# FFN down products as seven block products, with their sums on VectorE, and all operand buffers moved by 384 bytes

## The chip, the cores and the metric

The kernel runs on one core of a Trainium2 chip. Its metric is device time in microseconds (us). The engines in this text are TensorE (PE), VectorE (DVE), ScalarE (ACT), GpSimd (POOL) and the DMA queue that SyncE (SP) feeds.

## The reference

Three blocks for 256 tokens of width 1024: a sparse-attention layer and an MLA layer, each with a squared-ReLU MLP, and a hybrid mLSTM and windowed-attention layer, which ends in the FFN that this change is about. All is float32.

```python
hf = rmsnorm(x, norm_ffn_g)
x = x + (jax.nn.silu(hf @ w_gate) * (hf @ w_up)) @ w_down      # w_gate, w_up: 1024x2816; w_down: 2816x1024
...
return rmsnorm(x, norm_final_g)
```

## The kernel before

All of it is one program with an instruction list per engine, written out by hand, that wait for one another on semaphores. Weights stream through in chunks of 128x2048 float32 (1 MB), each loaded into one of two `raw` buffers. ACT copies a chunk to a rounded fp32r value (`whi`, helper `split_one`, L1566), and DVE (L2125, helper `low_part`) or POOL (L1535) writes the rest, raw minus whi, to `wlo`. Activations are split the same way, and each product is three matmuls on PE (high by high, high by low, low by high; lines 548 to 550 in `three`).

The last FFN runs over D_FF2 = 2816 in 11 steps of 256 columns: a gate chunk g(p), an up chunk u(p) and a down chunk d(p). PE makes g(p+1) and u(p+1), each 2 tiles x 8 k x 3 = 48 matmuls of 256 columns (`wide_step`), and then the down products of step p, 2 token blocks x 2 halves x 2 k x 3 = 24 matmuls of 512 columns (`ffn_down`, `down_products`). The down products of all steps add up in banks 0 to 3 of PSUM. Gate tiles lie in banks 4 and 5, up tiles in 6 and 7, two of each so that DVE can read one while PE fills the other. The steps run in a loop of 4 turns with two steps each, with two steps ahead of it and one behind.

Between the products, DVE multiplies the gate by the norm's row scale (L2763), ACT applies SiLU (L2073), DVE multiplies by up (L2769), ACT copies the rounded hidden value to `xC` (L2077), and DVE writes its rest (L2773). The norm ahead of the FFN is late: the products begin on gained but unscaled values, and DVE makes the scales while PE works on g0 and u0 (L2158 to L2164). PE spreads them to a row (L1343), and ACT copies that. The residual sum takes the same scales at the end (`residual_add`, L2138), followed by the final norm (ACT squares at L1552, POOL gain products at L1543, DVE scaling at L2183).

SP issues the chunk loads in order. Each waits until the low part of the chunk that was in its `raw` buffer is written.

## Time and profile before

| | us |
|---|---|
| median of 3 runs (lowest, highest) | 1139.35 (1138.67, 1140.9) |
| the profiled execution | 1141.42 |
| its span | 1139.6 |
| PE busy in the span | 1112.0 |
| DVE busy | 707.6 |
| ACT busy | 583.6 |
| POOL busy | 142.6 |

The profiled execution took 1.8 us more than its span, and 2.1 us more than the median. Sums made on the trace are differences within the span, so they can be taken from the median as they are. Busy time of PE counts matmuls that overlap in the pipeline. How fast it goes is read from the distance between the starts of two matmuls.

### The profile page before, as it was taken

To read this page: it belongs to the slowest core of one execution; us is meant where nothing else is said; L and a number is where in the kernel's file an instruction comes from. 1 tells how busy PE (TensorE), PEld (TensorE's weight loads), DVE (VectorE), ACT (ScalarE), POOL (GpSimd) and SP (SyncE) were. 2 spreads that over 40 slices of the span, in tenths; PEclk is the share of its full clock that TensorE was granted. 3 is DMA by queue.
4 is the path that set the end of the run, shared out by engine and by line. 5 is a ranking of instruction groups with operands and counts; after the bars stand their busy time and mean duration, and the time that the engine had idled before them with its cause. 6 is when DMAs were issued, how large, how long until landed. Compare 5 with 4: busy or idle time off the path is not lost.

```text
span 1139.6 us, 17781 instructions
## 1 busy us (share of the span) xinstructions
PE 1112.0 (98%) x7033; PEld 984.8 (86%) x7033; DVE 707.6 (62%) x997; ACT 583.6 (51%) x767; POOL 142.6 (13%) x105
## 2 busy tenths in 40 slices
PE   8899999999998999999999999999999999999997
PEld 7767888888887888888888999898899989999996
DVE  5764565565668646565656878566587566554554
ACT  5565544444579554444455546455555346443443
POOL 3543300000265240000030000000000011000001
PEclk9999999999999999999999999999999999999999
DMA  7917565555442236556545654436643545656552
GB/s 216 306 54 186 182 198 188 200 190 184 118 137 88 98 111 222 191 186 201 189 156 185 204 171 149 132 128 223 203 159 120 185 148 160 221 175 194 189 172 89
DMA packets 138782, 193.96 MB, mean 170 GB/s; under 512 B 7147, under 2 KB 112840, under 8 KB 138716
## 3 DMA queue, kind: packets, MB, share of 16 engines
q1 hardware_dynamic: 126796, 181.92, 48.4%
q10 hardware_dynamic: 11312, 11.05, 3.6%
q8 instruction: 45, 0.74, 0.3%
q0 software_dynamic: 608, 0.08, 0.1%
q14 instruction: 21, 0.17, 0.0%
HBM read 191.90 MB, written 6.37 MB: 174 GB/s over the span
## 4 chain that ended last, share of the span: by engine, by line
PE 83%; ACT 6%; DVE 5%; issue 2%; DMA 2%; POOL 0%; ACTq 0%; DVEq 0%; POOLq 0%
PE psum L548 20%; PE psum L549 20%; PE psum L550 20%; PE psum L709 11%; PE psum L710 5%; ACT arena L1552 3%; PE psum L637 2%; ACT whi L1566 2%; DVE wlo L2125 1%; DMA raw<-in_a_w_in 1%; PE psum L1264 1%; PE psum L668 1%; PE psum L1237 1%; DVE arena L2566 1%; DMA raw<-in_b_w_o 0%
## 5 line engine op out<-in xcount | busy, mean ns | idle before, releaser
L1566 ACT ACTIVATE whi<-raw 128x2048 fp32r<-128x2048 f32 (+2 forms) x174 | 325.9, 1875 | 255.5 <-PE psum L550 172.5
L2125 DVE TENSOR_TENSOR wlo<-raw,whi 128x2048 fp32r<-128x2048 f32 (+1 forms) x149 | 337.5, 2267 | 184.1 <-ACT whi L1566 183.2
L548 PE MATMUL psum<-xA,whi 128*128 128x256 f32 x840 | 239.8, 285 | 2.7 <-DVE wlo L2125 1.7
L549 PE MATMUL psum<-xA,whi 128*128 128x256 f32 x840 | 237.6, 283 | 0.0
L550 PE MATMUL psum<-xA,wlo 128*128 128x256 f32 x840 | 237.5, 283 | 0.0
L1535 POOL TENSOR_TENSOR wlo<-raw,whi 128x288 fp32r<-128x288 f32 (+3 forms) x56 | 112.6, 2037 | 793.8 <-ACT whi L1566 793.5
L709 PE MATMUL psum<-xA,whi 128*128 128x512 f32 x512 | 183.0, 400 | 0.0
L548 PEld LDWEIGHTS psum<-xA,whi 128*128 128x128 f32 x840 | 160.3, 191 | 6.0 <-DVE wlo L2125 3.2
L549 PEld LDWEIGHTS psum<-xA,whi 128*128 128x128 f32 x840 | 160.4, 191 | 0.7
L550 PEld LDWEIGHTS psum<-xA,wlo 128*128 128x128 f32 x840 | 160.4, 191 | 0.1
L548 PE MATMUL psum<-whi,xC 128*128 128x512 f32 (+1 forms) x384 | 149.2, 389 | 1.1 <-DVE xC L2439 1.1
L549 PE MATMUL psum<-wlo,xC 128*128 128x512 f32 (+1 forms) x384 | 148.6, 387 | 0.0
L550 PE MATMUL psum<-whi,xC 128*128 128x512 f32 (+1 forms) x384 | 148.1, 386 | 0.0
L710 PE MATMUL psum<-xA,wlo 128*128 128x256 f32 x512 | 143.7, 281 | 0.0
L709 PEld LDWEIGHTS psum<-xA,whi 128*128 128x128 f32 x512 | 96.2, 188 | 24.9 <-DVE xA L2151 1.2
L548 PE MATMUL psum<-whi,xA 128*128 128x512 f32 (+1 forms) x256 | 100.1, 391 | 0.0
L549 PE MATMUL psum<-wlo,xA 128*128 128x512 f32 (+1 forms) x256 | 98.6, 385 | 0.0
L550 PE MATMUL psum<-whi,xA 128*128 128x512 f32 (+1 forms) x256 | 98.6, 385 | 0.0
L710 PEld LDWEIGHTS psum<-xA,wlo 128*128 128x128 f32 x512 | 96.7, 189 | 1.1
L548 PEld LDWEIGHTS psum<-whi,xC 128*128 128x128 f32 x384 | 72.1, 188 | 16.5 <-DVE xC L2439 1.1
L550 PEld LDWEIGHTS psum<-whi,xC 128*128 128x128 f32 x384 | 72.1, 188 | 14.4
L549 PEld LDWEIGHTS psum<-wlo,xC 128*128 128x128 f32 x384 | 72.1, 188 | 12.5
(269 smaller groups left out, 1339.7 us busy)
## 6 DMA issues: line engine op xcount, KB each, us to landing
raw<-in_w_in SPq DMA_DIRECT2D x42, 1024.0 KB, 4.9
raw<-in_mlp_w_up SPq DMA_DIRECT2D x32, 1024.0 KB, 5.4
raw<-in_mlp_w_down SPq DMA_DIRECT2D x32, 1024.0 KB, 4.8
raw<-in_w_gate SPq DMA_DIRECT2D x11, 1024.0 KB, 5.1
raw<-in_w_up SPq DMA_DIRECT2D x11, 1024.0 KB, 5.2
raw<-in_w_down SPq DMA_DIRECT2D x11, 1024.0 KB, 4.8
raw<-in_a_w_in SPq DMA_DIRECT2D x6, 1024.0 KB, 7.1
raw<-in_a_w_o SPq DMA_DIRECT2D x4, 1024.0 KB, 4.7
```

What stands on the lines that cost most here:

```text
L548: nc.tensor.matmul(out, lh, rh, start=start, stop=False, skip_group_check=skip)
L549: nc.tensor.matmul(out, lh, rl, start=False, stop=False, skip_group_check=skip)
L550: return nc.tensor.matmul(out, ll, rh, start=False, stop=stop, skip_group_check=skip)
L637: ins = nc.tensor.transpose(out[0:m, n * P:n * P + P], src, ident[:, :])
L668: ins = nc.tensor.transpose(out[:, (2 * i + blk) * P:(2 * i + blk) * P + P], hres[:, blk, k * P:k * P + P], ident[:, :])
L709: nc.tensor.matmul(out, hi[:, k, nt * P:nt * P + P], xA[:, :, k, :], start=k == 0, stop=False)
L710: ins = nc.tensor.matmul(out[:, 0:SEQ], lo[:, k, nt * P:nt * P + P], xA[:, 0, k, :], start=False, stop=k == KT - 1)
L1237: ins = nc.tensor.matmul(psum[:, bank[f"C.h{h}.S{n}"], x * w:x * w + w], C["qa"][r0:r0 + 64, g * 4 + i, blk * P:blk * P + P], C["ka"][r0:r ...
L1535: ins = T(wlo[c % N_SPLIT][:, at:at + step], raw[c % N_RAW][:, at:at + step], f(whi[c % N_SPLIT][:, at:at + step]), ALU.subtract)
L1552: ins = nc.scalar.activation(out, in_, func, **kw)
L1566: nc.scalar.activation(whi[c % N_SPLIT][:, 0:n], raw[c % N_RAW][:, 0:n], ACT.Copy).then_inc(hi_sem, 1)
L2125: V.tensor_tensor(wlo[c % N_SPLIT][:, 0:n], raw[c % N_RAW][:, 0:n], f(whi[c % N_SPLIT][:, 0:n]), ALU.subtract).then_inc(lo_sem["dve"], 1)
```

## The change

Each down step multiplies 2x2 blocks of the hidden values (2 k by 2 token blocks of 128) by 2x2 blocks of the weights (2 k by 2 halves of 512). The changed kernel makes these of seven block products where there were eight, M1 to M7, in steps 0 to 9; step 10 keeps its eight (`four_products`). Each product has one PSUM bank of its own, 1 to 7, over all ten steps, so gate and up tiles have only bank 0 from step 2 on. The table `seven` names bank, hidden block and weight block.

- DVE makes the sums of hidden blocks (`hidden_sums`, 3 instructions) and of weight blocks (`weight_sums`, 3), and their low parts. Block 0 of the weights needs no split of its own.
- The down chunks leave the ring of `raw` buffers and have two of their own, as have their split parts (`down_split`, over the arena). The hidden values go to `down_raw` and `xB`.
- PE's turn is g(p+1), three of the products of step p, u(p+1), the other four. u waits until DVE has scaled the gate out of bank 0, and the next g until DVE has read u.
- The weight sums of step 0 are made before the norm; the second gate tile is scaled after the first turn's sums.
- At the end `seven_sums` on DVE adds M1, M5, M6 and M7 to the residual in their combinations; M2, M3 and M4 are in banks 3, 2 and 1, where the eight products of step 10 join them.
- `fill_front` is 96 floats ahead of all buffers. `raw0` was at byte 16512 of a partition and is at 16896. The buffers `whi`, `wlo`, `hres`, `xA`, `xB`, `xC` and the arena, whose addresses were 128 bytes over a multiple of 512, lie at multiples of 512 bytes.

```diff
+sb("fill_front", [P, 96])
 raw = [sb(f"raw{i}", [P, SLOT]) for i in range(N_RAW)]
...
-arena = sb("arena", [P, 20480])
-xC = sb("xC", [P, 3072], F32R)
+sb("fill_middle", [P, 8])
+with nc.sbuf_tensor("xC", [P, 3072], F32R) as xC:
+    pass
+down_raw = sb("down_raw", [P, 3072])
+with nc.sbuf_tensor("arena", [P, 20480], F32) as arena:
+    pass
+down_split = sb("down_split", [P, 4 * 3584], F32R)
...
+down_hi = [down_split[:, 7168 * j:7168 * j + 3584] for j in range(2)]
+down_lo = [down_split[:, 7168 * j + 3584:7168 * j + 7168] for j in range(2)]
+wsum = area(14336, 4, 512)
+raw_bufs = [raw[0][:, :], raw[1][:, :], down_raw[:, 0:SLOT], area(16384, SLOT)]
+hidden = down_raw[:, SLOT:SLOT + 1024]
+xB_flat = xB[:, :, :, :].rearrange("p s k n -> p (s k n)")
+hidden_hi = [xB_flat[:, 2048 * j:2048 * j + 1024] for j in range(2)]
+hidden_lo = [xB_flat[:, 2048 * j + 1024:2048 * j + 2048] for j in range(2)]
+gate_buf, rs_row = area(18432, 512), area(18944, SEQ)
+fin_g = area(19456, D)
...
+seven = {"M1": (4, 1, 0), "M2": (3, 3, 2), "M3": (2, 7, 1), "M4": (1, 2, 6),
+         "M5": (5, 4, 3), "M6": (6, 5, 5), "M7": (7, 6, 4)}
+SEVEN = ("M1", "M6", "M7", "M5", "M2", "M3", "M4")
...
+def seven_products(s, p, order, loop=None, start=False, closing=None, part=None):
+    def count(at):
+        return along([at(x) for x in loop[0]], loop[1]) if loop else at(p)
+    if part in (None, 0):
+        pe.wait_ge(down_low_raw, count(lambda x: whole_count(s, x)))
+        pe.wait_ge(down_low_sum, count(lambda x: sums_count(s, x)))
+        pe.wait_ge(hidden_low, count(lambda x: whole_count(s, x)))
+    wh, wl = [w[p % 2].rearrange("p (a n) -> p a n", n=512) for w in (down_hi, down_lo)]
+    xh, xl = [v[p % 2].rearrange("p (a n) -> p a n", n=P) for v in (hidden_hi, hidden_lo)]
+    for m in order:
+        b, x, w = seven[m]
+        ins = three(psum[:, b, :], xh[:, x, :], xl[:, x, :], wh[:, w, :], wl[:, w, :], start, True, True)
+        if closing and b >= 4:
+            close_bank(ins, f"{closing}.{m}")
+    if part in (None, 1):
+        ins.then_inc(seven_done, 1)
+def four_products(s, n):
+    p = down_steps[s] - 1
+    pe.wait_ge(down_low_raw, whole_count(s, p))
+    pe.wait_ge(hidden_low, whole_count(s, p))
+    wh, wl = [w[p % 2][:, 0:2 * D].rearrange("p (k n) -> p k n", n=D) for w in (down_hi, down_lo)]
+    xh, xl = [v[p % 2].rearrange("p (a n) -> p a n", n=P) for v in (hidden_hi, hidden_lo)]
+    for blk in range(NB):
+        for half in range(2):
+            b = 2 * blk + half
+            for k in range(2):
+                cols_ = slice(512 * half, 512 * half + 512)
+                ins = three(psum[:, b, :], xh[:, 2 * k + blk, :], xl[:, 2 * k + blk, :],
+                            wh[:, k, cols_], wl[:, k, cols_], b == 0 and k == 0, k == 1, True)
+            close_bank(ins, f"{n}.res{b}")
...
-def ffn_down(c, lo_count, h_count, j2, start, last):
+wide_step("g1", 5, low[index["ffn.g1"]], None)
+wide_step("u1", 7, low[index["ffn.u1"]], None)
+open_seven("F")
+pe.wait_ge(gate_scaled, 2)
+seven_products(2, 0, ("M2", "M3", "M4", "M1", "M5", "M6"), None, True, None, 0)
+pe.wait_ge(hidden_step, hidden_count(2, 1, 1))
+seven_products(2, 0, ("M7",), None, True, None, 1)
+def free_up(p):
+    return hidden_count(2, p, 1)
+def ffn_turn(p, loop=None, closing=None, cut_at=3):
+    def count(at):
+        return along([at(x) for x in loop[0]], loop[1]) if loop else at(p)
+    wide_step(f"g{p + 1}", 0, count(lambda x: low[index[f"ffn.g{x + 1}"]]), (hidden_step, count(free_up)))
+    seven_products(2, p, SEVEN[:cut_at], loop, False, closing, 0)
+    wide_step(f"u{p + 1}", 0, count(lambda x: low[index[f"ffn.u{x + 1}"]]),
+              (gate_scaled, count(lambda x: x + 2)))
+    seven_products(2, p, SEVEN[cut_at:], loop, False, closing, 1)
+ffn_turn(1)
+with pe.Fori(0, 3) as r:
+    for q in range(2):
+        ps_ = [2 + 2 * y + q for y in range(3)]
+        ffn_turn(ps_[0], (ps_, r))
+ffn_turn(8)
+ffn_turn(9, None, "F", 2)
+four_products(2, "F")
...
 @block.sync
-for x in range(c, c + 8):
-    static(x)
+static(index["ffn.d0"])
+for x in range(3):
+    for kind in ("gu", "gud", "gu")[x]:
+        static(index[f"ffn.{kind}{x}"])
+with sp.Fori(0, 4) as r:
+    for q in range(2):
+        for kind, view, first in (("d", wd, 2), ("g", wg, 3), ("u", wu, 3)):
+            js = [first + 2 * y + q for y in range(4)]
+            ring([index[f"ffn.{kind}{j}"] for j in js], view, js, kind == "d", r)
+static(NC - 1)
...
 @block.scalar
...
+    nc.scalar.activation(down_hi[p % 2][:, 0:1536], raw_bufs[raw_of[c]][:, 512:SLOT],
+                         ACT.Copy).then_inc(down_high_raw, 1)
+if "sum" in parts:
+    act.wait_ge(down_sum, count(lambda x: 3 * sums_count(s, x)))
+    nc.scalar.activation(down_hi[p % 2][:, 1536:3584], wsum.rearrange("p a n -> p (a n)"),
+                         ACT.Copy).then_inc(down_high_sum, 1)
...
+    nc.scalar.activation(hidden_hi[p % 2][:, v], hidden[:, v], ACT.Copy).then_inc(hidden_high, 1)
...
+def ffn_step(p, loop=None):
+    hidden_copy(2, p, loop)
+    down_high(2, p + 1, ahead_of(loop))
+    gate_silu(p + 1, ahead_of(loop))
+    for w in "gu":
+        if loop:
+            split_loop([index[f"ffn.{w}{x + 2}"] for x in loop[0]], loop[1])
+        elif p < NF - 2:
+            split_static(index[f"ffn.{w}{p + 2}"])
+gate_silu(0)
+down_high(2, 1, None, ("raw",))
+hidden_copy(2, 0)
+down_high(2, 1, None, ("sum",))
+gate_silu(1)
+for w in "gu":
+    split_static(index[f"ffn.{w}2"])
+ffn_step(1)
...
 @block.vector
+def hidden_sums(s, p, loop=None):
+    def step(k, ins):
+        ins.then_inc(hidden_step, 1)
+        at = [hidden_count(s, x, k) for x in (loop[0] if loop else (p,))]
+        dve.wait_ge(hidden_step, along(at, loop[1]) if loop else at[0])
+    x = hidden.rearrange("p (a n) -> p a n", n=P)
+    step(2, V.tensor_tensor(x[:, 6, :], x[:, 0, :], x[:, 1, :], ALU.subtract))
+    step(3, V.tensor_tensor(x[:, 4:6, :], x[:, 0::6, :], x[:, 2:3, :].to_broadcast([P, 2, P]), ALU.subtract))
+    V.tensor_tensor(x[:, 7, :], x[:, 3, :], x[:, 5, :], ALU.add).then_inc(hidden_step, 1)
+def weight_sums(s, p, loop=None):
+    def step(k, ins):
+        ins.then_inc(down_sum, 1)
+        at = [3 * sums_count(s, x) - 3 + k for x in (loop[0] if loop else (p,))]
+        dve.wait_ge(down_sum, along(at, loop[1]) if loop else at[0])
+    c = down_chunk(s, p)
+    at = [landed[down_chunk(s, x)] for x in (loop[0] if loop else (p,))]
+    dve.wait_ge(raw_sem[raw_of[c]], along(at, loop[1]) if loop else at[0])
+    b = raw_bufs[raw_of[c]].rearrange("p (a n) -> p a n", n=512)
+    step(1, V.tensor_tensor(wsum[:, 0:2, :], b[:, 0:1, :].to_broadcast([P, 2, 512]), b[:, 1:3, :], ALU.add))
+    step(2, V.tensor_tensor(wsum[:, 2, :], b[:, 1, :], wsum[:, 1, :], ALU.add))
+    V.tensor_tensor(wsum[:, 3, :], b[:, 3, :], wsum[:, 2, :], ALU.add).then_inc(down_sum, 1)
+def sum_low(s, p, loop=None):
+    at = [sums_count(s, x) for x in (loop[0] if loop else (p,))]
+    dve.wait_ge(down_high_sum, along(at, loop[1]) if loop else at[0])
+    V.tensor_tensor(down_lo[p % 2][:, 1536:3584], wsum.rearrange("p a n -> p (a n)"),
+                    f(down_hi[p % 2][:, 1536:3584]), ALU.subtract).then_inc(down_low_sum, 1)
+def raw_low(s, p, loop=None):
+    at = [whole_count(s, x) for x in (loop[0] if loop else (p,))]
+    dve.wait_ge(down_high_raw, along(at, loop[1]) if loop else at[0])
+    a, n = (0, SLOT) if p == down_steps[s] - 1 else (512, 1536)
+    V.tensor_tensor(down_lo[p % 2][:, 0:n], raw_bufs[N_RAW + p % 2][:, a:a + n], f(down_hi[p % 2][:, 0:n]),
+                    ALU.subtract).then_inc(down_low_raw, 1)
+def hidden_rest(s, p, loop=None):
+    at = [whole_count(s, x) for x in (loop[0] if loop else (p,))]
+    dve.wait_ge(hidden_high, along(at, loop[1]) if loop else at[0])
+    v = slice(0, 512) if p == down_steps[s] - 1 else slice(P, 1024)
+    V.tensor_tensor(hidden_lo[p % 2][:, v], hidden[:, v], f(hidden_hi[p % 2][:, v]),
+                    ALU.subtract).then_inc(hidden_low, 1)
+def seven_sums(n):
+    def scaled(b, half, src, scale, then=None):
+        h = hres[:, b, 512 * half:512 * half + 512]
+        run(V.scalar_tensor_tensor(h, src, scale[:, b:b + 1], h, ALU.mult, ALU.add), then)
+    run(V.tensor_scalar(minus_scale, late_scale, -1.0, None, ALU.mult))
+    dve.wait_ge(*read[f"{n}.M1"])
+    dve.wait_ge(*full[f"{n}.M6"])
+    run(V.tensor_tensor(wsum[:, 1, :], psum[:, 6, :], wsum[:, 0, :], ALU.add), read[f"{n}.M6"])
+    scaled(1, 1, wsum[:, 0, :], late_scale)
+    dve.wait_ge(*full[f"{n}.M7"])
+    run(V.scalar_tensor_tensor(wsum[:, 2, :], psum[:, 7, :], -1.0, wsum[:, 1, :], ALU.mult, ALU.add), read[f"{n}.M7"])
+    scaled(1, 0, wsum[:, 1, :], minus_scale)
+    dve.wait_ge(*full[f"{n}.M5"])
+    scaled(1, 0, psum[:, 5, :], late_scale)
+    scaled(0, 0, psum[:, 5, :], late_scale, read[f"{n}.M5"])
+    scaled(0, 0, wsum[:, 2, :], minus_scale)
+    scaled(0, 1, wsum[:, 2, :], late_scale)
...
+if n == "F":
+    mean_square(n, 0)
+    mean_square(n, 1)
+    sum_low(2, 0)
...
+def gate_scale(p, loop=None):
+    dve.wait_ge(gu_full, count(lambda x: 2 * x + 1, p, loop))
+    V.tensor_tensor(gate_buf.rearrange("p (a b) -> p a b", b=SEQ),
+                    psum[:, (4, 5)[p] if p < 2 else 0, :].rearrange("p (a b) -> p a b", b=SEQ),
+                    rs_row.unsqueeze(1).to_broadcast([P, 2, SEQ]), ALU.mult).then_inc(gate_scaled, 1)
+def product(p, loop=None):
+    dve.wait_ge(gu_full, count(lambda x: 2 * x + 2, p, loop))
+    dve.wait_ge(silu_done, count(lambda x: x + 1, p, loop))
+    if p:
+        dve.wait_ge(hidden_low, count(lambda x: whole_count(2, x - 1), p, loop))
+    V.tensor_tensor(hidden[:, 0:512], psum[:, (6, 7)[p] if p < 2 else 0, :], gate_buf,
+                    ALU.mult).then_inc(hidden_step, 1)
+    dve.wait_ge(hidden_step, count(lambda x: hidden_count(2, x, 1), p, loop))
+def ffn_step(p, loop=None):
+    product(p, loop)
+    hidden_sums(2, p, loop)
+    if p < NF - 2:
+        weight_sums(2, p + 1, ahead_of(loop))
+    hidden_rest(2, p, loop)
+    raw_low(2, p + 1, ahead_of(loop))
+    gate_scale(p + 1, ahead_of(loop))
+    if p < NF - 2:
+        sum_low(2, p + 1, ahead_of(loop))
+    for w in "gu":
+        if loop:
+            low_loop([index[f"ffn.{w}{x + 2}"] for x in loop[0]], loop[1])
+        elif p < NF - 2:
+            low_part(index[f"ffn.{w}{p + 2}"])
+gate_scale(0)
+weight_sums(2, 1)
+product(0)
+hidden_sums(2, 0)
+gate_scale(1)
+hidden_rest(2, 0)
+raw_low(2, 1)
+sum_low(2, 1)
+for w in "gu":
+    low_part(index[f"ffn.{w}2"])
+ffn_step(1)
+with dve.Fori(0, 3) as r:
+    for q in range(2):
+        ps_ = [2 + 2 * y + q for y in range(3)]
+        ffn_step(ps_[0], (ps_, r))
+for p in (8, 9):
+    ffn_step(p)
+product(NF - 1)
+hidden_rest(2, NF - 1)
+seven_sums("F")
```

The first place is DVE in one turn of the FFN (the second step, which is written out). Before, `gate scale`, `product`, the hidden value's rest and three chunk rests:

```order
L2763 TENSOR_TENSOR arena<-psum,arena 128x512
L2769 TENSOR_TENSOR arena<-psum,arena 128x512
L2125 TENSOR_TENSOR wlo<-raw,whi 128x2048
L2773 TENSOR_TENSOR xC<-arena,xC 128x512
L2125 TENSOR_TENSOR wlo<-raw,whi 128x2048 x2
```

And of the changed kernel, from the product (L3037) on:

```order
L3037 TENSOR_TENSOR down_raw<-psum,arena 128x512
L2318 TENSOR_TENSOR down_raw<-down_raw 128x128
L2319 TENSOR_TENSOR down_raw<-down_raw 128x256
L2320 TENSOR_TENSOR down_raw<-down_raw 128x128
L2333 TENSOR_TENSOR arena<-down_raw 128x1024
L2334 TENSOR_TENSOR arena<-down_raw,arena 128x512
L2335 TENSOR_TENSOR arena<-down_raw,arena 128x512
L2357 TENSOR_TENSOR xB<-down_raw,xB 128x896
L2349 TENSOR_TENSOR down_split<-down_raw,down_split 128x1536
L3028 TENSOR_TENSOR arena<-psum,arena 128x512
L2341 TENSOR_TENSOR down_split<-arena,down_split 128x2048
L2301 TENSOR_TENSOR wlo<-raw,whi 128x2048 x2
```

The six sums (L2318 to L2335) are new, and the down chunk's rest has become two pieces (L2349, L2341) of 1536 and 2048 columns.

The second place is DVE between the last projection's rests and the norm of the FFN. Before:

```order
L2125 TENSOR_TENSOR wlo<-raw,whi 128x2048 x2
L2141 TENSOR_TENSOR hres<-psum,hres 128x512 x4
L2151 SCALAR_TENSOR_TENSOR xA<-psum,vecs,xA 128x256 x8
L2125 TENSOR_TENSOR wlo<-raw,whi 128x2048
L2158 TENSOR_TENSOR st<-st 128x1
```

Changed:

```order
L2301 TENSOR_TENSOR wlo<-raw,whi 128x2048 x2
L2333 TENSOR_TENSOR arena<-down_raw 128x1024
L2334 TENSOR_TENSOR arena<-down_raw,arena 128x512
L2335 TENSOR_TENSOR arena<-down_raw,arena 128x512
L2349 TENSOR_TENSOR down_split<-down_raw,down_split 128x1536
L2390 TENSOR_TENSOR hres<-psum,hres 128x512 x4
L2406 SCALAR_TENSOR_TENSOR xA<-psum,vecs,xA 128x256 x8
L2301 TENSOR_TENSOR wlo<-raw,whi 128x2048
```

Four instructions for chunk d0 stand ahead of the residual sums, and behind the chunk's rest the 2048-column piece of d0 (L2341) stands between the mean squares and the scales.

The third place is DVE at the end. Before, from the last hidden value's rest on:

```order
L2773 TENSOR_TENSOR xC<-arena,xC 128x512
L2138 SCALAR_TENSOR_TENSOR hres<-psum,st,hres 128x512 x3
L2173 TENSOR_SCALAR st<-st 128x1
L2178 RECIPROCAL st<-st 128x1
L2183 TENSOR_SCALAR arena<-arena,st 128x512
```

Changed:

```order
L2357 TENSOR_TENSOR xB<-down_raw,xB 128x512
L2366 TENSOR_SCALAR st<-st 128x2
L2369 TENSOR_TENSOR arena<-psum,arena 128x512
L2364 SCALAR_TENSOR_TENSOR hres<-arena,st,hres 128x512
L2372 SCALAR_TENSOR_TENSOR arena<-psum,arena 128x512
L2364 SCALAR_TENSOR_TENSOR hres<-arena,st,hres 128x512
L2364 SCALAR_TENSOR_TENSOR hres<-psum,st,hres 128x512 x2
L2364 SCALAR_TENSOR_TENSOR hres<-arena,st,hres 128x512 x2
L2387 SCALAR_TENSOR_TENSOR hres<-psum,st,hres 128x512 x3
L2430 TENSOR_SCALAR st<-st 128x1
```

Nine instructions (L2366, L2369, L2372 and six of L2364) stand between the last hidden value and the residual sums.

## Rows read from the trace of the kernel before

**Rows 1.** The page: busy time, share of the span and instructions of each engine.

```profile
PE 1112.0 (98%) x7033; PEld 984.8 (86%) x7033; DVE 707.6 (62%) x997; ACT 583.6 (51%) x767; POOL 142.6 (13%) x105
```

**Rows 2.** Windows: stretch, its length, busy us (instructions) by engine, PEclk, DMA share, GB/s.

```profile
1001.95:1018.93 16.98, 16.98 (x122) 16.02 (x121) 8.86 (x6) 6.78 (x5) 0.00 (x0) 1.00 0.56 186
...
1120.80:1139.60 18.80, 11.08 (x50) 8.84 (x48) 8.27 (x15) 6.96 (x15) 3.86 (x3) 0.94 0.15 56
```

**Rows 3.** Timeline of PE, FFN matmuls: start us, us, engine, line, tiles, shape.

```profile
967.99 0.40 PE L548 MATMUL psum<-whi,xC 128*128 128x512 f32 x1
...
1018.93 0.40 PE L548 MATMUL psum<-whi,xC 128*128 128x512 f32 x1
...
1024.40 0.28 PE L548 MATMUL psum<-xA,whi 128*128 128x256 f32 x1
...
1131.49 0.39 PE L550 MATMUL psum<-whi,xC 128*128 128x512 f32 x1
```

**Rows 4.** Timeline of DVE in one turn; in brackets what ended its idle time.

```profile
1019.13 0.69 DVE L2763 TENSOR_TENSOR arena<-psum,arena 128x512 f32<-128x512 f32 x1 [1.52 <-PE psum L550]
...
1022.33 2.29 DVE L2125 TENSOR_TENSOR wlo<-raw,whi 128x2048 fp32r<-128x2048 f32 x1 [1.02 <-ACT whi L1566]
1024.54 0.69 DVE L2773 TENSOR_TENSOR xC<-arena,xC 128x512 fp32r<-128x512 f32 x1
```

**Rows 5.** Timeline of ACT in the same turn.

```profile
1019.86 0.63 ACT L2073 ACTIVATE arena<-arena 128x512 f32<-128x512 f32 x1 [4.57 <-DVE arena L2763]
1020.39 1.90 ACT L1566 ACTIVATE whi<-raw 128x2048 fp32r<-128x2048 f32 x1
```

**Rows 6.** Timeline at the FFN's start: DVE, POOL, ACT and SP's queue.

```profile
926.52 4.49 DVE L2125 TENSOR_TENSOR wlo<-raw,whi 128x2048 fp32r<-128x2048 f32 x2 [1.26 <-ACT whi L1566]
938.09 0.69 DVE L2141 TENSOR_TENSOR hres<-psum,hres 128x512 f32<-128x512 f32 x1 [7.07 <-PE psum L550]
...
948.19 2.29 DVE L2125 TENSOR_TENSOR wlo<-raw,whi 128x2048 fp32r<-128x2048 f32 x1 [1.31 <-ACT whi L1566]
...
955.86 2.29 DVE L2125 TENSOR_TENSOR wlo<-raw,whi 128x2048 fp32r<-128x2048 f32 x1 [1.45 <-ACT whi L1566]
...
936.05 9.18 POOL L1535 TENSOR_TENSOR wlo<-raw,whi 128x2048 fp32r<-128x2048 f32 x2 [338.80 <-ACT whi L1566]
...
958.84 1.28 ACT L2073 ACT_TABLE_LOAD   x1 [1.77 <-DVE arena L2763]
...
945.26 0.37 SPq L1378 DMA_DIRECT2D raw<-in_w_up  x1
```

**Rows 7.** Timeline of DVE at the end of the program.

```profile
1130.56 0.75 DVE L2138 SCALAR_TENSOR_TENSOR hres<-psum,st,hres 128x512 f32<-128x512 f32 x1 [0.61 <-PE psum L550]
...
1132.06 0.98 DVE L2183 TENSOR_SCALAR arena<-arena,st 128x512 f32<-128x512 f32 x1
1133.08 0.75 DVE L2138 SCALAR_TENSOR_TENSOR hres<-psum,st,hres 128x512 f32<-128x512 f32 x1
1133.93 0.69 DVE L2193 TENSOR_TENSOR arena<-hres,arena 128x512 f32<-128x512 f32 x1
1134.66 0.49 DVE L2183 TENSOR_SCALAR arena<-arena,st 128x512 f32<-128x512 f32 x1
```

**Rows 8.** Timeline of PE: moving operands of 288 columns, then stationary ones of 36.

```profile
313.57 0.30 PE L548 MATMUL psum<-whi,xA 128*128 128x288 f32 x1
...
313.97 0.29 PE L548 MATMUL psum<-whi,xA 128*128 128x288 f32 x1
...
314.76 0.29 PE L548 MATMUL psum<-whi,xA 128*128 128x288 f32 x1
...
315.16 0.30 PE L548 MATMUL psum<-whi,xA 128*128 128x288 f32 x1
...
681.31 0.28 PE L548 MATMUL psum<-xA,whi 128*36 128x256 f32 x1
681.43 0.28 PE L549 MATMUL psum<-xA,whi 128*36 128x256 f32 x1
```

329 lines of the change are left out of this document (177 added, 152 removed).

## The prediction

> **What bounds the kernel now.** I read the page first. PE is busy 98% of the span [rows 1]. Windows of the last FFN come next: in one turn PE is busy all of its 16.98 us at a granted clock of 1.00, and DVE 8.86 us of it [rows 2]. PE's timeline says what a turn is made of. The 24 down matmuls start at 1018.93 and the next chunk's at 1024.40, so they take 5.47 us, 0.228 each. The other 96, of gate and up, take 16.98 - 5.47 = 11.51 us, 0.120 each [rows 2, 3]. DVE's timeline shows what the other engines cost there: each of DVE's instructions waited for PE or ACT, and nothing on PE waited for them [rows 4]. So the FFN is bound by PE up to its last matmul at 1131.49 [rows 3]. From there DVE and ACT finish the residual, the norm and the output, until 1139.6.
>
> **Matmuls removed.** Steps 0 to 9 lose 3 of 24 matmuls each: 30 x 0.228 = 6.8 us of PE time. This is the most that the change can give through PE. It shortens a turn to 11.51 + 21 x 0.228 = 16.30 us.
>
> **What DVE gets.** A 512-column instruction takes 0.69 us and a 2048-column one 2.29 [rows 4], so a column costs 1.04 ns. From this line: 128 columns 0.29, 256 columns 0.42, 896 columns 1.09, 1024 columns 1.22, 1536 columns 1.76. Behind an independent instruction the next starts 0.08 before the end (1022.33 to 1024.54 is 2.21 for 2.29 [rows 4]). Behind a dependent one it starts 0.04 to 0.10 after it (1133.93 to 1134.66, 1133.08 to 1133.93 [rows 7]). A turn of DVE is then: product 0.69; hidden sums 0.29 + 0.42 + 0.29; weight sums 1.22 + 0.69 + 0.69; hidden rest 1.09; 1536-column rest 1.76; gate scale 0.69; 2048-column rest 2.29; two chunk rests 4.58. The sum is 14.7 us, 5.8 more than now. With overlap and dependent gaps the queue takes 14.3 us from product to product if it waits for nothing. It does wait, since gate scale and product come behind PE's tiles. Taking g's end as time 0 and DVE's start 0.20 behind PE's (1018.93 to 1019.13 [rows 3, 4]): gate scale at 0.2; SiLU to 1.6 and the split of g to 3.4 on ACT [rows 5]; DVE's 2048-column rest to 3.1, g's rest from 3.5, u's rest to 7.9. PE makes three products until 2.05 and u until 7.8, so the product starts at 8.05 and bank 0 is free at 8.9. PE wants it at 10.55, after its last four products. Then sums and rests run until about 15.2, ahead of the next gate at 16.3. DVE has about 1.2 us to spare per turn and PE's wait for bank 0 about 1.7. I take both waits at nothing. The broadcast and strided operands of the sums are not in the trace in these shapes; bounds are nothing (L2763 reads a broadcast row in 0.69, as others do [rows 4]) and twice the 3.6 us of the six, where the turn would be bound by DVE (rival B). I take nothing, by L2763.
>
> **Entry.** DVE is idle from 926.52 + 4.49 = 931.0 to 938.09 [rows 6]. The weight sums of d0 and its 1536-column rest are 1.22 + 0.69 + 0.69 + 1.76 = 4.4 us and end at 935.5, so they cost nothing. The two mean squares stand together now, 2.29 of the sums' rest follows them, and then the scales. From 948.19 + 2.29 = 950.5, with 1.0 for the means, 2.3, and 1.0 for reciprocals and scales (estimates by the gaps above), the scales are there at 954.8. PE needs them at the end of u0, which is 967.99 - 2 x 5.76 - 0.4 = 956.1: covered by 1.3 us. u1's rest then ends at 957.1, where it ended at 955.86 + 2.29 = 958.15. The load of d1 is queued behind u1's at 945.26 [rows 6] and has 12 us to land, where the page has 4.8 us for such a load.
>
> **The first turn has a stall.** DVE from 957.1: gate scale to 957.8, weight sums of d1 to 960.4 (they cover ACT's table load of 1.28 [rows 6] and SiLU), product to 961.1, hidden sums to 962.2, second gate (g1 ends at 962.2) to 963.1, hidden rest to 964.3, the two rests of d1 to 968.2, rests of g2 and u2 to 972.6, and only then the product of step 1, to 973.25. That product frees u1's bank 7, which M7 needs. PE ends u1 at 967.99 and six products at 967.99 + 18 x 0.228 = 972.1, so M7 waits until 973.35. The stall is 1.3 us. All that precedes the product on DVE stands in front of it, so each 0.1 us there adds to it; bounds are 0.8 and 2.5.
>
> **Up to u10.** g2 starts at 973.35 + 0.68 = 974.05. Eight turns of 16.30 end at 1104.45; g10, two products (M1, M6) and u10 take 5.76 + 1.37 + 5.76, so u10 ends at 1117.3. Before, it ended at 1018.93 + 6 x 16.98 = 1120.8. The gain here is 3.5 us: 21 matmuls (4.8) less the stall.
>
> **The end moves to DVE.** PE has 15 + 24 matmuls behind u10 and would stop at 1117.3 + 39 x 0.228 = 1126.2, 5.5 us earlier than before. But DVE makes the last product and rest (0.69 each, with ACT's copy of 0.6 between them) until 1119.6 and then `seven_sums`: a tiny one of 0.15, one of 0.69 and seven of 0.75 [rows 7], in a chain with 0.04 to 0.10 between them. That is 6.4 us (bounds 6.1 to 7.0, and nothing to be gained below), so the first residual sum starts at 1126.0, when all four banks but the last are full. The three sums follow each other at 0.67. The third starts at 1127.3, and was at 1130.56 [rows 7]. ACT's squares, which used to fit between PE's banks, now come 0.45 late behind it (two of 0.63 and 0.19 in a row against one). The end moves from 1139.6 by -3.25 + 0.45 = -2.8 us. So of 6.8 us, 1.3 stay in the first turn and 2.7 in DVE's chain at the end.
>
> **Buffers at multiples of 512 bytes.** The trace has fp32r matmuls at several offsets. The 288-column operands step by 1152 bytes, so the four k of a chunk start 128, 256, 384 and 0 bytes over a multiple of 512. Three matmuls of the first k take 313.57 to 313.97, and of the fourth, which is at 0, 314.76 to 315.16: 0.40 both [rows 8]. With 36-column stationary operands at steps of 144 bytes the distance is 0.12, as with 128 [rows 8]. I take nothing. Stationary operands of 128 columns at 0 are in no row. Bounds: 3 ns either way on 7033 matmuls [rows 1], 21 us. The Trainium skill, page "SBUF — State Buffer", section "Operand start alignment", asks only that an operand start at a multiple of its element size and calls this a matter of legality, not speed; by it too the move is worth nothing.
>
> **Sum.** The span goes to 1139.6 - 2.8 = 1136.8, the profiled execution from 1141.42 to 1138.6, and the median of the runs from 1139.35 to 1136.5. What can be told from no change here is about 0.2%, 2.3 us, so I forecast a gain just above that.
>
> **Rival A: less is left.** Same mechanism, but the first turn's stall is near 2.5 us and the chain at the end near 7.0, since a chain of dependent instructions takes every gap in full. The time would be 1136.5 + 1.2 + 0.6 = 1138.3. For it: DVE is in both places the engine that PE waits for. Against it: the gaps in the rows are small.
>
> **Rival B: DVE bounds the turn (slower).** Six short sums in a row wait for one another, with register values to be made between them inside the loop. The change stops paying when eight turns lose its 2.8 us, at 16.65 per turn, where I count 15.1 for DVE. The point is 1.5 us more per turn, 0.15 on each of the ten new or split instructions. At 2.5 more the turn is 17.6, 8 x 1.3 = 10.4 us are lost and the time is 1146.9. For it: DVE's load in the FFN goes from 8.9 to 14.7 us of 16.3. Against it: dependent gaps of 0.04 to 0.10 [rows 7].
>
> **Rival C: POOL holds DVE up at the entry.** POOL's rests of g0 and u0 run from 936.05 for 9.18 us [rows 6]. A DVE instruction beside POOL took 0.98 at 1132.06 where its like took 0.49 at 1134.66 [rows 7]. If d0's 1536-column rest starts behind 936.05 and waits for POOL's first instruction (4.6 us), the residual sums, the norm and PE's g0 come 2.3 us late: 1138.8. It has 2.4 us of room (it starts at 933.7), so only a late d0 brings it. The Trainium skill ("SBUF — State Buffer", "Who interferes with whom") says that a VectorE instruction with two SBUF inputs and a GpSimd one that reads SBUF exclude each other for their full length; this rest and the weight sums are of that kind.
>
> **Rival D: the aligned buffers make matmuls faster.** 3 ns on each matmul would give 1136.5 - 21 = 1115.5. Nothing in the rows speaks for it beyond the one case they don't have.
>
> **Chances.** Forecast 0.57, A 0.24, B 0.07, C 0.04, D 0.06, and 0.02 for slower matmuls. Forecast and D make up most of "faster by over 0.2%" (0.48 + 0.06, and 0.04 for a stall or chain smaller than I think): 0.58. Within 0.2%: 0.33 (A, C, the forecast's upper edge). Slower: 0.09. The range leaves out D and B: 1134.3 (no stall, and 1 us less at the end) to 1139.3 (A and C together, nearly).
>
> **What would show it.** A turn of 16.3 us with the clock at 1.00, and distances of 0.228 and 0.120, show the PE terms. One PE wait of about 1.3 us ahead of M7 in the first turn shows the stall. DVE's nine instructions in a row behind the last hidden rest, with PE's end near 1126, show the tail. DVE idle of about 1 us ahead of each gate scale shows that B is false; none, with PE waiting for `hidden_step` or `down_low_raw`, shows it true. The prediction is wrong if matmul distances change with the addresses, if PE waits inside the loop, or if anything ahead of 931 moves.

## The result, and the profile after

The changed kernel takes 1146.51 us (median of 20 runs, 1137.9 to 1151.69), the kernel before, run beside it, 1140.74 (1137.24 to 1143.44). The ratio is 1.005, with a 95% interval of 1.0036 to 1.0064: slower by half a per cent, where I had forecast 0.25% faster. The profiled execution took 1148.72 us, with a span of 1146.9.

The windows of the changed kernel are one turn, the end from u10's last product, and the stretch at the entry in which TensorE stands (stretch, length, busy us and instructions by engine, PEclk, DMA share, GB/s):

```profile
990.36:1006.67 16.31, 16.31 (x118) 15.46 (x117) 14.27 (x13) 8.48 (x6) 0.00 (x0) 1.00 0.57 205
1127.85:1146.90 19.05, 9.03 (x41) 7.15 (x39) 13.16 (x23) 6.32 (x14) 3.86 (x3) 0.83 0.15 56
944.00:956.00 12.00, 5.49 (x27) 5.20 (x26) 10.20 (x12) 3.91 (x9) 3.32 (x1) 0.72 0.77 263
```

The turn is 16.31 us where it was 16.98 [rows 2], PE is busy in all of it, and the end takes 19.05 where it took 18.80. Only the third row is new. Between 944 and 956 PE is busy for less than half of the time, and the mean granted clock is 0.72: part of the stretch ran at 1.2 GHz and not at 2.4. Before the gap PE had been busy throughout. Who was late shows in the timelines of ACT, DVE, POOL and PE there (start, duration, engine, line, tiles, shape; in brackets the idle time ahead and what ended it):

```profile
926.69 3.72 ACT L1688 ACTIVATE whi<-raw 128x2048 fp32r<-128x2048 f32 x2
936.20 1.92 ACT L1688 ACTIVATE whi<-raw 128x2048 fp32r<-128x2048 f32 x1 [5.79 <-DMA raw<-in_w_gate]
939.55 1.92 ACT L1688 ACTIVATE whi<-raw 128x2048 fp32r<-128x2048 f32 x1 [1.44 <-DMA raw<-in_w_up]
941.38 1.47 ACT L1708 ACTIVATE down_split<-down_raw 128x1536 fp32r<-128x1536 f32 x1
...
935.10 0.69 DVE L2335 TENSOR_TENSOR arena<-down_raw,arena 128x512 f32<-128x512 f32 x1
942.88 6.06 DVE L2349 TENSOR_TENSOR down_split<-down_raw,down_split 128x1536 fp32r<-128x1536 f32 x1 [7.08 <-ACT down_split L1708]
948.86 2.47 DVE L2390 TENSOR_TENSOR hres<-psum,hres 128x512 f32<-128x512 f32 x4
...
938.20 9.12 POOL L1657 TENSOR_TENSOR wlo<-raw,whi 128x2048 fp32r<-128x2048 f32 x2 [338.67 <-ACT whi L1688]
...
943.93 0.39 PE L613 MATMUL psum<-whi,xA 128*128 128x512 f32 x1
950.83 3.65 PE L731 MATMUL psum<-ident,hres 128*128 128x128 f32 x16 [6.51 <-issue]
954.13 0.56 PE L611 MATMUL psum<-xA,whi 128*128 128x256 f32 x1
```

ACT made the high copy of d0's raw columns (L1708) last, behind the splits of g0 and u0, for whose transfers it had waited 5.79 and 1.44 us. DVE had finished the weight sums at 935.79, waited 7.08 us for that copy, and began the 1536-column rest at 942.88. POOL's second rest began at about the same time. The rest took 6.06 us instead of 1.76, until 948.94, and POOL's two took 9.12 together, as ever [rows 6]: DVE's instruction ran when POOL's was over. The four residual sums stood behind it, so PE's transposes started at 950.83 and not at 944.16. They and the norm took 3.30 us to g0 (950.83 to 954.13), part of it at half clock. In the kernel before it had been 1.81:

```profile
941.98 2.06 PE L668 MATMUL psum<-ident,hres 128*128 128x128 f32 x16
943.79 0.36 PE L548 MATMUL psum<-xA,whi 128*128 128x256 f32 x1
```

The whole account, from the profiled executions: 2.2 us had gone by before the stretch (the rests of co2 and co3 start at 928.72, before at 926.52 [rows 6]); 6.7 us more until the transposes; 1.5 us between them and g0; -5.3 us from g0 to the last matmul at 1136.49 (182.4 for 187.7); and +2.3 us from there to the end (10.44 for 8.14). The sum is +7.4; the spans differ by 7.3. The 2.2 us are a difference between executions and not between kernels (E10); without them it is 5.2, where the medians differ by 5.8. The last two terms together are -3.0: what the change does to the loop and the end is what I had forecast.

The end, on DVE:

```profile
1129.52 0.69 DVE L2357 TENSOR_TENSOR xB<-down_raw,xB 128x512 fp32r<-128x512 f32 x1 [0.77 <-ACT xB L1725]
1130.12 0.16 DVE L2366 TENSOR_SCALAR st<-st 128x2 f32<-128x2 f32 x1
1130.32 0.69 DVE L2369 TENSOR_TENSOR arena<-psum,arena 128x512 f32<-128x512 f32 x1
...
1134.92 1.54 DVE L2364 SCALAR_TENSOR_TENSOR hres<-arena,st,hres 128x512 f32<-128x512 f32 x2
1136.49 2.07 DVE L2387 SCALAR_TENSOR_TENSOR hres<-psum,st,hres 128x512 f32<-128x512 f32 x3
```

The nine instructions of `seven_sums` take 6.37 us in a row, from 1130.12 to 1136.49, and the residual sums wait behind them.

### The profile page after: what moved, and what is told of

It is laid out like the page before. It is cut to its first block, busy times and chain, and to the rows that moved or that the text cites. A ratio compares the mean times of both kernels' runs of the same rounds, so it can differ in the third digit from the quotient of the medians.

```text
span 1146.9 us, 17845 instructions
## 1 busy us (share of the span) xinstructions
PE 1107.4 (97%) x7003; PEld 982.0 (86%) x7003; DVE 771.9 (67%) x1076; ACT 600.7 (52%) x778; POOL 142.6 (12%) x105
## 3 DMA queue, kind: packets, MB, share of 16 engines
HBM read 191.90 MB, written 6.37 MB: 173 GB/s over the span
## 4 chain that ended last, share of the span: by engine, by line
PE 79%; DVE 10%; ACT 6%; issue 3%; DMA 2%; ACTq 0%; DVEq 0%
PE psum L611 19%; PE psum L612 18%; PE psum L613 18%; PE psum L814 11%; PE psum L815 5%; ACT arena L1674 3%; PE psum L700 2%; ACT whi L1688 2%; DVE wlo L2301 2%; DVE psum L2756 1%; DMA raw<-in_a_w_in 1%; PE psum L731 1%; PE psum L1369 1%; DVE down_split L2349 1%; DVE arena L2586 1%
## 5 line engine op out<-in xcount | busy, mean ns | idle before, releaser
L1688 ACT ACTIVATE whi<-raw 128x2048 fp32r<-128x2048 f32 (+2 forms) x163 | 303.7, 1871 | 201.5 <-PE psum L613 130.2
L2301 DVE TENSOR_TENSOR wlo<-raw,whi 128x2048 fp32r<-128x2048 f32 (+1 forms) x138 | 311.5, 2264 | 128.4 <-ACT whi L1688 127.4
L611 PE MATMUL psum<-whi,xC 128*128 128x512 f32 (+1 forms) x296 | 114.9, 388 | 1.1 <-DVE xC L2696 1.1
L612 PE MATMUL psum<-wlo,xC 128*128 128x512 f32 (+1 forms) x296 | 114.3, 386 | 0.0
L613 PE MATMUL psum<-whi,xC 128*128 128x512 f32 (+1 forms) x296 | 114.1, 385 | 0.0
L1799 ACT ACTIVATE arena<-psum 128x512 f32<-128x512 f32 x32 | 19.1, 597 | 102.3 <-PE psum L815 102.3
L611 PEld LDWEIGHTS psum<-whi,xC 128*128 128x128 f32 x296 | 55.6, 188 | 13.1 <-DVE xC L2696 1.1
L613 PEld LDWEIGHTS psum<-whi,xC 128*128 128x128 f32 x296 | 55.6, 188 | 10.9
```

The lines of the kernel that those rows point to most:

```text
L611: nc.tensor.matmul(out, lh, rh, start=start, stop=False, skip_group_check=skip)
L612: nc.tensor.matmul(out, lh, rl, start=False, stop=False, skip_group_check=skip)
L613: return nc.tensor.matmul(out, ll, rh, start=False, stop=stop, skip_group_check=skip)
L1688: nc.scalar.activation(whi[split_of[c]][:, 0:n], raw_bufs[raw_of[c]][:, 0:n], ACT.Copy).then_inc(hi_sem, 1)
L1799: nc.scalar.activation(half_buf[:, j2, :].rearrange("p (a b) -> p a b", b=SEQ), psum[:, 4 + 2 * j2:6 + 2 * j2, SEQ:512], ACT.Copy).then_in ...
L2301: V.tensor_tensor(wlo[split_of[c]][:, 0:n], raw_bufs[raw_of[c]][:, 0:n], f(whi[split_of[c]][:, 0:n]), ALU.subtract).then_inc(lo_sem["dve"], 1)
```

## The experiments

Each kernel was timed against the kernel before on the same chip; a ratio is to that, with its 95% interval. It can differ a little from the quotient of the medians. E1, E2, E5; then E3, E4, E6, E7; then the rest shared a chip. The theory (H): the entry's order on ACT makes DVE's rest meet POOL's. The rival that the expectations call theory C, which is not rival C of the prediction: the loss is in the clock early in the program, or spread over the turns.

**E1: d0's high copy ahead of g0's split.** One ACT instruction moves.

```diff
+            split_to("co3")
+            down_high(2, 0, None, ("raw",))
             ahead("co3")
...
             c0 = first_of["ffn"]
-            down_high(2, 0, None, ("raw",))
             split_to(c0)
```

> The changed kernel with one ScalarE instruction moved: the high copy of d0's 1536 raw columns stands behind co3's split and ahead of the splits of g0 and u0, where the engine sat idle for 5.8 us. Theory H (the loss is at the entry of the feed-forward part: d0's high copy came at 941.38, so VectorE's 1536-column rest began beside GpSimd's second rest, took 6.06 us instead of about 1.8 and held the residual sums): the rest runs at about 935.8 to 937.6, ahead of GpSimd's first rest at 938.2, TensorE's 6.5 us wait ahead of the late transposes goes, so does the half-clock stretch behind it, and the time falls by 6 to 8.5 us from 1146.5, to 1138 to 1140.5, at or below the kernel before (1140.7). Theory C (the loss came with the half-clock stretches near the start of the program, or is spread over the turns): the time stays within 1144 to 1147.

Measured: 1138.41 us, ratio 0.9969 (0.9944 to 0.9993), 2.7 us under the 1141.14 of the kernel before beside it by the medians. Its DVE and POOL at the entry:

```profile
933.89 1.75 DVE L2350 TENSOR_TENSOR down_split<-down_raw,down_split 128x1536 fp32r<-128x1536 f32 x1
938.46 0.69 DVE L2391 TENSOR_TENSOR hres<-psum,hres 128x512 f32<-128x512 f32 x1 [2.82 <-PE psum L613]
...
936.37 9.18 POOL L1657 TENSOR_TENSOR wlo<-raw,whi 128x2048 fp32r<-128x2048 f32 x2 [338.64 <-ACT whi L1688]
```

The rest takes 1.75 us and ends 0.7 ahead of POOL's first; DVE then waits for PE, and PE goes from the last product into the transposes without a gap. From g0 to the last matmul it takes 182.23 us, as in the changed kernel (182.36), so the loss was not in the turns. Nor was it in the clock early in the program: between 34 and 50 us the granted clock is 0.79 in the changed kernel and 0.79 in E1 too, and 0.89 in the kernel before and in E10, the changed kernel's second profile. So 0.8% of time hung on the place of one instruction on an engine that was idle.

**E2: the rest behind the norm instead.** The same meeting, avoided on DVE.

```diff
             weight_sums(2, 0)
-            raw_low(2, 0)
             late_norm("F", "co", c0 + 2)
             low_part(c0 + 3)
+            raw_low(2, 0)
```

> The changed kernel with the same collision taken away from VectorE's side: d0's 1536-column rest stands behind the late norm and behind u1's rest, where the first turn's gate scale would otherwise be waited for. ScalarE's order is that of the changed kernel. Theory H: the residual sums are no longer held, the wait of 6.5 us goes and the time is 1138 to 1141, with up to 1.8 us of it given back in the first turn, where VectorE is late by 0.9 us already. Theory C: 1144 to 1147. If it was ScalarE's copy itself (1.5 us) that held up the norm, and not the rest on VectorE, this run stays slow while the one with the copy moved gets fast.

Measured: 1141.24 us, ratio 1.0009 (0.9984 to 1.0033), at the top of what H gave and clear of the changed kernel's interval. The wait ahead of the transposes is gone, though ACT's copy is as late as in the changed kernel (at 941.50): it was the rest on DVE and not the copy. More was given back than the 1.8 us that I allowed, and PE's first M7 (of E2, then of E1) shows where:

```profile
976.77 0.73 PE L611 MATMUL psum<-down_split,xB 128*128 128x512 f32 x1 [2.51 <-DVE down_raw L3037]
```

```profile
973.50 0.50 PE L611 MATMUL psum<-down_split,xB 128*128 128x512 f32 x1 [0.86 <-DVE down_raw L3038]
```

The wait grew by 1.65 us (2.90 between two starts for 1.25), and behind it the clock fell for a while. The windows of E2, then of E1:

```profile
970.00:982.00 12.00, 9.49 (x48) 8.13 (x47) 11.83 (x12) 6.52 (x5) 0.00 (x0) 0.86 0.59 197
```

```profile
970.00:982.00 12.00, 11.14 (x72) 9.89 (x71) 11.39 (x13) 5.27 (x5) 0.00 (x0) 1.00 0.73 262
```

From g0 to the last matmul E2 takes 185.40 us, 3.2 more than E1: 1.65 of wait, and some 1.5 behind it, which I put down to the lower level.

**E3: the meeting alone, put into the kernel before.** It gets a DVE subtraction of the same size whose result nobody reads. A first form of it, e3_before_held, gave no result; this is the second, e3b_before_held.

```diff
             c0 = first_of["ffn"]
+            dve.wait_ge(hi_sem, c0 + 2)
+            flat = hres[:, :, :].rearrange("p a b -> p (a b)")
+            unread = xB[:, 0, 0:6, :].rearrange("p k n -> p (k n)")
+            run(V.tensor_tensor(unread, flat[:, 0:1536], flat[:, 512:2048], ALU.subtract))
             late_norm("F", "co", c0 + 2)
```

> The kernel before with one suspected cost added: a VectorE subtraction of 128x1536 from SBUF to SBUF (its result is read by nobody) ahead of the residual sums, waiting for u0's high copy, which ends at 938.9 while GpSimd's rest of g0 runs (936.05 to 940.68) and u0's follows (940.63 to 945.23). Theory H (VectorE and GpSimd don't run such instructions side by side; the residual sums are held behind it): the instruction takes 3.5 us if it gets its turn between GpSimd's two, 6 to 8 us if it runs behind the second; the residual sums start at 942.5 or at 947 instead of 938.1, TensorE waits 2 or 6 us ahead of the late transposes, and the time goes up by 2 to 9 us, to 1143 to 1150. Theory C (no such holding up): VectorE has 7 us idle there, the instruction costs its 1.8 us at most, and the time stays under 1142.

Measured: 1142.54 us, ratio 1.0024 (1.0005 to 1.0043): 1.2 us slower by the medians and 2.7 by the ratio. DVE, POOL and PE at the entry:

```profile
941.29 3.37 DVE L2760 TENSOR_TENSOR xB<-hres 128x1536 fp32r<-128x1536 f32 x1 [8.07 <-ACT whi L1566]
944.70 1.89 DVE L2141 TENSOR_TENSOR hres<-psum,hres 128x512 f32<-128x512 f32 x3
...
938.43 10.64 POOL L1535 TENSOR_TENSOR wlo<-raw,whi 128x2048 fp32r<-128x2048 f32 x2 [339.62 <-ACT whi L1566]
...
943.95 0.39 PE L550 MATMUL psum<-whi,xA 128*128 128x512 f32 x1
946.68 1.94 PE L668 MATMUL psum<-ident,hres 128*128 128x128 f32 x16 [2.35 <-issue]
```

This is the cheap outcome. DVE came while POOL's first instruction ran and got its turn between POOL's two: 3.37 us, of which about 1.6 is waiting, and POOL's pair took 10.64 instead of 9.18. The time alone doesn't decide: it is at the low end of what H gave, or just under it, and over C's 1142 only because the kernel before was 0.6 us slower here than the 1140.7 from which both bounds were set. The trace does decide: the instruction took 3.37 us and not 1.76, and PE waited 2.3 us ahead of the transposes, where the kernel before has no wait. The granted clock behind that gap, 2.73 us between two starts, stayed at 1.00 (944 to 960).

**E4 and E8: where the buffers lie.** Both start from E1. E4 takes out `fill_front` and widens `fill_middle`, so that raw, whi, wlo, hres, xA and xB lie at 128 bytes over a multiple of 512, while xC, down_raw, arena and down_split stay at multiples. (The expectation of E4 says that all were lower; these four were not.) E8 takes out `fill_front` only, and all lie at 128 over, as in the kernel before.

```diff
-        sb("fill_front", [P, 96])
-        sb("fill_middle", [P, 8])
+        sb("fill_middle", [P, 104])
```

> The changed kernel with d0's high copy ahead of g0's split (1138.4 when measured, ratio to before 0.9969), and all of its large buffers 384 bytes lower, so that they begin at 128 over a multiple of 512 as in the kernel before. Prediction's step (alignment is worth nothing): ratio 0.995 to 0.999, matmul distances 0.120 and 0.227 us and the DVE rest 2.29 us as they are. Rival (the place of the buffers is worth something to TensorE's or VectorE's reads): slower by 5 us or more, ratio above 1.001.

> The changed kernel with d0's high copy ahead of g0's split, and now every large buffer 384 bytes lower, xC, down_raw, arena and down_split too. In the run before this one only raw, whi, wlo, hres, xA and xB were lower; its 512-wide matmuls on whi with xC and on down_split with xB, whose two operands then lay at 128 and at 0 over a multiple of 512, came every 0.232 us instead of 0.228, those on xA with whi (both at 128) stayed at 0.236, and the ratio to before was 1.0019 instead of 0.9969. If it is the two operands' places against each other, all distances are as in the base again (0.228 for whi with xC, 0.229 for down_split with xB), and the ratio is 0.995 to 0.999. If it is a place off the multiple of 512 itself, whi with xC stays at 0.232 or rises, and the ratio is 1.000 to 1.004.

Measured: E4 1141.89 us, ratio 1.0019 (1.0002 to 1.0037); E8 1136.15, ratio 0.9958 (0.9937 to 0.9978); E1 had 0.9969. First and last of the same 24 matmuls in an earlier MLP, of E1, E4 and E8:

```profile
450.49 0.40 PE L611 MATMUL psum<-whi,xC 128*128 128x512 f32 x1
...
455.73 0.39 PE L613 MATMUL psum<-whi,xC 128*128 128x512 f32 x1
```

```profile
441.99 0.39 PE L610 MATMUL psum<-whi,xC 128*128 128x512 f32 x1
...
447.32 0.39 PE L612 MATMUL psum<-whi,xC 128*128 128x512 f32 x1
```

```profile
450.52 0.40 PE L610 MATMUL psum<-whi,xC 128*128 128x512 f32 x1
...
455.76 0.39 PE L612 MATMUL psum<-whi,xC 128*128 128x512 f32 x1
```

23 distances take 5.24, 5.33 and 5.24 us: 0.2278, 0.232 and 0.2278 each. In the loop the mean distance of the matmuls on down_split and xB is 0.2293, 0.2326 and 0.2293. Those on xA and whi, whose buffers moved together, keep theirs: 0.2278, 0.2275 and 0.2278 where whi is the stationary operand and nothing is waited for (distances under 0.3 us). So what matters is where the two operands lie against each other, and not whether they lie on a multiple of 512: E8 has E1's distances with both at 128. I tried one shift of one against the other only (384 bytes), so after how many bytes it repeats isn't shown, and how the chip comes to it stays open.

**E11: the alignment alone.** The kernel before with `fill_front`: all large buffers from 128 over to multiples of 512.

```diff
+        sb("fill_front", [P, 96])
         raw = [sb(f"raw{i}", [P, SLOT]) for i in range(N_RAW)]
```

> The alignment alone: the kernel before with its large buffers, all at 128 over a multiple of 512, moved up by 384 bytes to multiples of 512. Prediction's step: nothing, ratio 0.998 to 1.002, matmul distances 0.120 and 0.227 us. Rival (multiples of 512 are faster to read): under 0.997, the mean distance of the 512-wide ones below 0.2278.

Measured: 1142.57 us, ratio 1.0012 (0.999 to 1.0034). From first to last start the same 24 matmuls take 5.24 us, 0.2278 each, in both kernels. The move as the change makes it does nothing to the matmuls, and nothing to the time that is clear of the noise.

**E5: PE kept busy in the gap.**

```diff
             residual("co", xA, lambda j: done[f"C.m{j}.lo"])
+            g0 = index["ffn.g0"]
+            pe.wait_ge(hi_sem, high[g0])
+            pe.wait_ge(read_sem[4], uses[4])
+            for _ in range(25):
+                nc.tensor.matmul(psum[:, 4, :], whi[split_of[g0]][:, 0:P], whi[split_of[g0]][:, 0:512], start=True, stop=True)
```

> The changed kernel with 25 matmuls 128x512 (5.7 us at 0.227, products of g0's high copy with itself into a bank that g0 starts anew) between the last output product and the late transposes, where TensorE waits 6.5 us. The wait for VectorE is not touched. It separates the two parts of the entry's loss: if the half-clock stretch (949.1 to 955.9) comes from the idle stretch and costs what its matmuls show (0.21 us instead of 0.12 for the 256-wide ones), it goes and the time falls by 1 to 2.5 us, to 1144 to 1145.5, while the norm still starts late. If the clock's part is the larger one, it falls by over 4 us, to under 1142.5. If the clock falls without an idle stretch, nothing changes (1146 to 1147).

Measured: 1144.51 us, ratio 1.003 (1.0009 to 1.0051). The interval overlaps that of the changed kernel, and the profile turned out to show another thing:

```profile
942.96 1.76 DVE L2354 TENSOR_TENSOR down_split<-down_raw,down_split 128x1536 fp32r<-128x1536 f32 x1 [6.98 <-ACT down_split L1713]
944.64 1.88 DVE L2395 TENSOR_TENSOR hres<-psum,hres 128x512 f32<-128x512 f32 x3
...
938.40 10.79 POOL L1662 TENSOR_TENSOR wlo<-raw,whi 128x2048 fp32r<-128x2048 f32 x2 [338.74 <-ACT whi L1693]
...
950.02 1.91 PE L731 MATMUL psum<-ident,hres 128*128 128x128 f32 x16
951.80 0.35 PE L611 MATMUL psum<-xA,whi 128*128 128x256 f32 x1
```

DVE and POOL met at the same point, and here DVE went first: its rest took 1.76 us, and POOL's pair 10.79 instead of 9.12. The residual sums were done at 947.1, and PE went on with its 25 dummies until 950.0, nearly 3 us longer, which cost this execution most of what it would have gained. So the clock's share can't be read from its time. It can be read from the rows: the clock held while PE was fed (its window from 935 to 958 has a granted clock of 1.00, the changed kernel's 0.85), and from the transposes to g0 it took 1.78 us, where the changed kernel took 3.30 with the clock down. That is the 1.5 us of the account.

```profile
935.00:958.00 23.00, 22.98 (x129) 19.85 (x129) 10.36 (x16) 13.96 (x18) 10.79 (x2) 1.00 0.56 196
```

```profile
935.00:958.00 23.00, 16.49 (x84) 14.58 (x82) 12.77 (x16) 12.27 (x14) 9.12 (x2) 0.85 0.56 192
```

**E10: the changed kernel once more.**

> The changed kernel unchanged, for its time on this chip beside the others and for a second look at its entry. Theory R (VectorE's rest and GpSimd's second rest are ready within 0.1 us of each other, and which of them goes first differs from execution to execution): the ratio is 1.003 to 1.007 again; if in this profile VectorE goes first, its rest takes about 1.8 us, GpSimd's 6.2, TensorE waits some 2.2 us instead of 6.5, and this execution's time is 4 to 6 us under the 1148.7 of the first look; if GpSimd goes first, it is as the first look.

Measured: 1145.04 us (1140.65 to 1151.46), ratio 1.004 (1.0018 to 1.0063).

```profile
925.37 4.49 DVE L2301 TENSOR_TENSOR wlo<-raw,whi 128x2048 fp32r<-128x2048 f32 x2 [1.26 <-ACT whi L1688]
...
939.62 6.04 DVE L2349 TENSOR_TENSOR down_split<-down_raw,down_split 128x1536 fp32r<-128x1536 f32 x1 [7.18 <-ACT down_split L1708]
```

POOL went first again. With this kernel's two profiles and E5's, whose program is the same up to PE's dummies, the meeting went POOL's way twice and DVE's once. The kernel's 20 runs lie 14 us apart (1137.9 to 1151.69) and those before beside it 6 apart, but the kernel before, which has no such meeting, lay 12 apart on the chip of E3 (1138.09 to 1150.09). So the spread says nothing of who goes first, and no profile of the unchanged program shows DVE first. The first row settles the 2.2 us: the co rests start at 925.37 here, in the first profile at 928.72 and before at 926.52 [rows 6]. That difference is one between executions, not between kernels. It also answers the expectation, which had put an execution with POOL first at the first profile's 1148.72: this one took 1144.73 and had lost as much to the meeting, but it came to the entry 3.35 us earlier.

**E6, E7 and E9: the end.** All start from E1. E6 puts `seven_sums` ahead of product(10), into DVE's idle time, and four of the seven products instead of two ahead of u10. E7 also moves product(1) ahead of the rests of g2 and u2. E9 is E7 with M5 behind u10 again, and its two sums behind product(10)'s rest. Of E9's edit:

```diff
-            ffn_turn(9, None, "F", 2)
+            ffn_turn(9, None, "F", 3)
...
             sum_low(2, 1)
+            product(1)
             for w in "gu":
...
+            later_sums = seven_sums("F")
             product(NF - 1)
             hidden_rest(2, NF - 1)
-            seven_sums("F")
+            later_sums()
```

> The same base (d0's high copy ahead of g0's split) with the end's sums moved: in the last turn the products M1, M6, M7 and M5 all stand ahead of u10's instead of two of them, and VectorE's nine instructions of seven_sums (6.4 us) stand ahead of product(10), in the 6.4 us from 1111.5 to 1117.95 in which that engine was idle. If the end is bound by VectorE's sums behind product(10), as the profile of that base shows (residual sums in a row from 1126.4), the four residual sums follow TensorE's four closing products one by one, the last at about 1127.1 instead of 1130.2, and the time falls by 2.5 to 3.5 us against the base's 1138.4. If the sums run into product(10) instead (they can start at 1112.7, when M1's copy is done), product(10) comes up to 1.5 us late and TensorE with it, and the gain is 1 to 2 us.

> The kernel with the end's sums moved, and product(1) ahead of the rests of g2 and u2 on VectorE instead of behind them. TensorE waited 0.9 us for product(1) ahead of M7 of the first turn. If that wait is on the path that sets the end, the time falls by another 0.9 us (0.6 to 1.3) below the one with the end's sums alone; rival: g2's rest is then late by the 0.7 us of product(1) and TensorE waits there instead, and nothing is gained.

> The kernel with the end's sums and product(1) moved, and one thing more: with four products ahead of u10 only 9 matmuls (2.1 us) covered product(10), its high copy and its rest, and TensorE waited 1.1 us ahead of the four closing products. M5 goes back behind u10 (12 matmuls cover), its two sums behind product(10)'s rest. From g0's first matmul to the last matmul 181.0 to 181.4 us instead of 182.05, from there to the end 8.1 to 8.5 as before, the time 0.5 to 1 us lower: 1137 to 1137.5, ratio 0.996. Rival: the two sums behind product(10) hold the residual sums back, and what TensorE gains the end loses.

Measured: E6 1138.53 us, ratio 0.9969 (0.9949 to 0.9989); E7 1138.03, 0.9968 (0.9952 to 0.9985); E9 1136.2, 0.995 (0.9929 to 0.9971), the fastest of all beside E8. Their intervals overlap E1's, so no step is shown by the time (of the 2.5 to 3.5 us expected of E6 it shows nothing), and the steps can only be told by the profiles. From g0 to the last matmul and from there to the end it takes 182.23 + 10.43 us in E1, 182.81 + 8.12 in E6, 182.05 + 8.11 in E7 and 181.09 + 8.18 in E9. The end's sums gain 2.3 us, under the 2.5 to 3.5 that I expected, and 0.6 of it goes into a new wait of PE for the last hidden rest, since only nine matmuls cover it; product(10) itself was not late. Product(1) gains its 0.8 us (the wait ahead of M7 is gone). E9 takes back the new wait: PE waits for nothing from 940 to the end, and from g0 to the end it is 3.4 us shorter than E1. DVE at the end of E9:

```profile
1117.97 2.33 DVE L2365 SCALAR_TENSOR_TENSOR hres<-arena,st,hres 128x512 f32<-128x512 f32 x3
1121.68 0.69 DVE L3041 TENSOR_TENSOR down_raw<-psum,arena 128x512 f32<-128x512 f32 x1 [1.38 <-PE psum L613]
1123.14 0.69 DVE L2358 TENSOR_TENSOR xB<-down_raw,xB 128x512 fp32r<-128x512 f32 x1 [0.77 <-ACT xB L1725]
1123.75 1.53 DVE L2365 SCALAR_TENSOR_TENSOR hres<-psum,st,hres 128x512 f32<-128x512 f32 x2
1125.80 0.75 DVE L2391 SCALAR_TENSOR_TENSOR hres<-psum,st,hres 128x512 f32<-128x512 f32 x1 [0.52 <-PE psum L613]
```

The residual sums wait for PE's banks again, and no longer for DVE's own queue.

## Why the prediction was wrong

**The step that failed** is the entry: "The weight sums of d0 and its 1536-column rest are 1.22 + 0.69 + 0.69 + 1.76 = 4.4 us and end at 935.5, so they cost nothing." I took the rest as a DVE instruction with nothing ahead of it but DVE's own queue. It reads ACT's high copy, and the prediction never gave that copy a start time. In the text of the program it stands ahead of `split_to(c0)`, but `ahead("co3")`, above it, had already split g0 and u0, and `split_to(c0)` does nothing. The transfers of g0 and u0 end that wait, at 936.20 and 939.55. So the rest was ready at 942.88 and not at 933.7.

**Rival C was the right mechanism with the wrong door and price.** It said that only a late d0 could bring it. d0 had landed by 933.12, when the weight sums read it; the copy was late. I priced it at POOL's first instruction (2.3 us late). In fact DVE met POOL's second and waited for nearly all of it, 4.3 us of the 6.7 (948.94 for 944.64); the other 2.4 are the late start alone. E3 shows the cheaper case that I had priced (2.3 us of PE's wait, and 1.2 us of time by the medians or 2.7 by the ratio). And I left out what a gap of that length does to the clock: 1.5 us more. I gave C 0.04. The Trainium skill ("SBUF — State Buffer", "Who interferes with whom"), which I had cited there, says that a VectorE instruction with two SBUF inputs and a GpSimd one that reads SBUF exclude each other for the full length of an instruction; 6.06 and 6.04 us for an instruction of 1.76, and 3.37 in E3, agree.

**What held.** E1 is the change without the collision: 2.7 us under the kernel before by the medians, where I forecast 2.8. So close a match is partly luck, since the interval of its ratio reaches from 0.8 to 6.4 us; the terms in the profile carry more weight. Point by point: the turn 16.31 for 16.30; matmul distances 0.120 and 0.2293 for 0.228, the latter 0.0013 more on 21 matmuls; the first turn's stall 0.86 us by the waits, 1.25 between the starts of two matmuls where 0.23 is usual, so 1.0 for 1.3; from u10 to the end 19.05 us for 19.5 (1117.3 to 1136.8); `seven_sums` 6.37 for 6.4. DVE idle ahead of the gate scale of a turn:

```profile
1006.67 0.69 DVE L3028 TENSOR_TENSOR arena<-psum,arena 128x512 f32<-128x512 f32 x1 [1.25 <-PE psum L613]
```

It had 1.25 us to spare where I counted 1.2, so rival B is false. Rival A is not needed: both of its terms came out at or under the forecast. Rival D, in the kernel as changed, is false too (E11). But the reason that I gave, that addresses are worth nothing, is not general: E4 shows 0.003 to 0.004 us on a matmul for a layout that the change happened not to use, and ratios of 1.0019 against 0.9969 and 0.9958 put that at 6 to 7 us over the program, with 2 us of uncertainty in each. The distances alone give about 4 us (816 matmuls on xC and 234 on down_split, 0.004 each). I had also read too much into the Trainium skill ("SBUF — State Buffer", "Operand start alignment"): it says that the rule on where an operand may start is about legality, not speed, and that its runs timed nothing. It doesn't say that a place costs no time, so neither E11 nor E4 speaks for or against it.

The sign that nothing ahead of 931 moves was of no use: the co rests start 3.35 us apart in two profiles of the same kernel (E10).

**The range** ended at 1139.3 and was said to cover A and C together, nearly. By their own prices they come to 1138.3 + 2.3 = 1140.6, so it didn't. With the order on ACT unread, it had no bound for the entry; even without the 2.2 us that belong to the execution, the account above is 5.2 us over the kernel before.

## What to carry to other kernels

When a moved instruction reads what another engine makes, give that producer a start time of its own from its queue, waits for transfers included, and find the helper calls above it that may have run its queue ahead. A VectorE and a GpSimd instruction that both read two SBUF operands should be kept apart by order, not by luck: when they became ready within about 0.1 us of each other, GpSimd went first in two profiles and VectorE in one (E5), and the loser waited for the whole of the other. A wait of TensorE can cost more than itself: between two starts, 1.25 us (E1) and 2.73 (E3) cost nothing besides, 2.90 (E2) and 6.90 cost some 1.5 us more each at the lower clock.

## What was not expected of the hardware

- 512-column fp32r matmuls came every 0.2278 us when both operands lay at a multiple of 512 bytes or both at 128 over one, and every 0.232 when one lay at a multiple and the other at 128 over (E1, E4, E8, E11).
- VectorE's 1536-column subtraction took 1.76 us alone, 6.04 and 6.06 when GpSimd's was first, 3.37 when it got its turn between two; and GpSimd's pair took 10.6 to 10.8 instead of 9.1 when VectorE was first or between (E3, E5).
- With no gap of TensorE at the entry, the granted clock there stayed at 1.00 (E1, E5); with one of 6.9 us between two starts it was 0.72 on the mean of 944 to 956. With one of 2.73 us it stayed at 1.00 (E3); with one of 2.90, in the first turn, it was 0.86 on the mean of 970 to 982 (E2).
